# A normalisation stage with three token buffers, four turned-piece buffers, rounding on ScalarE, bias lines amid the tiles and the first weights requested inside it

## The chip, the cores and the metric

One core of one Trainium2 chip runs the whole program: TensorE (PE in the profile), VectorE (DVE), ScalarE (ACT), GpSimd (POOL) and SyncE (SP), with on-chip memories SBUF and PSUM and 16 DMA engines to the chip's main memory. The metric is the device time of one execution in microseconds; below, "span" is the time from the first to the last instruction of one profiled execution.

## The reference

A hybrid attention layer for 512 prompt tokens and 8 x 8 sample tokens, width 2048. What matters here is its head: every token is normalised and multiplied with a wide weight matrix, and a small table of bias values is spread over distances.

```python
def rmsnorm(x, g):
    xf = x.astype(jnp.float32)
    y = xf * lax.rsqrt(jnp.mean(xf * xf, axis=-1, keepdims=True) + EPS)
    return (y * g.astype(jnp.float32)).astype(x.dtype)
p = project(rmsnorm(x, g_pre), w_in)        # 576 tokens x 2048 by 2048 x 7510
bias = table[t5_bucket(distance)]           # 32 buckets x 12 heads, over 4231 distances
```

After it come the attention over a paged cache of 8 sequences, that of the prompt, an output projection and a second normalisation.

## The kernel before

The program is a row of stages, each a function with its own block of five instruction lists, one for each engine, written out by hand. Every wait is a semaphore wait at a place in such a list, and an engine runs its list strictly in order. Between two stages stands a barrier of all engines and a clearing of the stage's semaphores (`Scope.clear`, L161 to L164).

`setup_and_norm` (L167 to L304) is the first stage. The tokens are five tiles m of 128 rows (the last, the samples, has 64). For each tile:

- SP loads `norm_x` (1 MB), in two buffers; tile m waits until the four pieces of tile m-2 have been turned (L199).
- ACT squares and sums it (L235), DVE scales the sum (L278), ACT takes Ln and Exp (L239, L241) for the inverse root, DVE multiplies the tile by it (L280).
- PE turns it in four pieces q of 4 x 128 columns by transposes (L256) into `norm_tp` (PSUM, two buffers).
- DVE multiplies a turned piece by the gain column and writes `norm_hT` (L294, SBUF, two buffers).
- POOL rounds the piece to the first half `h_hi` (L223) and subtracts it from the piece for the second half `h_lo` (L225). For the samples both go to `h_s`.

DVE's list has the norm of tile m+1 ahead of the pieces of tile m. After the tiles PE makes nine bias line pieces (L265) into `norm_lp` (two buffers), ACT copies them to `norm_line` (L244), and SP stores the line (L206) and waits for its landing. DVE meanwhile clips and reorders the page numbers (L298 to L304).

`project_in` (L307 to L454) is the second stage: 15 column chunks of 512 (the last is narrower), each in four quarters q of the 2048 rows. SP loads a quarter of the weights (`proj_w`, 1 MB, L344), DVE rounds it (`proj_w_hi`, L360), POOL subtracts (`proj_w_lo`, L391), and PE does three products for each token tile and k (L422 to L424, for the samples L415 and L418). ACT copies the sums out (L446).

Of the kernel before, what the change touches and what calls it, by code (L numbers as in the profile page):

```python
# [24 lines left out]
P = 128  # L25
# [135 lines left out]
def setup_and_norm(nc, io, kept, h_hi, h_lo, h_s):  # L161


    with ExitStack() as ctx:  # L164
        s = Scope(nc, ctx, "norm")
        x = s.sb("x", [P, 2, D])
# [13 lines left out]
        x_in = [s.sem(f"x_in{i}") for i in range(2)]  # L180
# [8 lines left out]

        @block.sync  # L190
        def _(sp):
            sp.dma_start(kept.consts[:], io.consts[:, 0:C_KEPT]).then_inc(consts_in, 16)
            sp.dma_start(choices[:].rearrange("p a n -> p (a n)"), io.consts[:, C_SELE:C_PM]).then_inc(choices_in, 16)
            for m in range(5):
                if m >= 2:

                    sp.wait_ge(turned, 4 * (m - 1))
                src = io.xp[m * P:(m + 1) * P, :] if m < 4 else io.xs
                sp.dma_start(x[0:rows[m], m % 2, :], src).then_inc(x_in[m % 2], 16)  # L199
# [4 lines left out]

# [5 lines left out]
        def _(pool):  # L210
            with nc.allow_non_contiguous_dma(reason="a small column"):
                pool.dma_start(gcol[:], io.norm_pre.rearrange("(k p) -> p k", p=P)).then_inc(gain_in, 16)
            pool.wait_ge(gain_in, 16)
            for m in range(5):
                for q in range(4):
# [6 lines left out]
                    pool.wait_ge(hT_written, n + 1)  # L222
                    pool.tensor_copy(hi, hT[n % 2][:, :, 0:rows[m]]).then_inc(hi_made, 1)  # L223
                    pool.wait_ge(hi_made, n + 1)
                    pool.tensor_tensor(lo, hT[n % 2][:, :, 0:rows[m]], hi, ALU.subtract).then_inc(lo_made, 1)  # L225

        @block.scalar
        def _(act):
            act.preload_act_table_set("natural_log_exp_and_others")
            for m in range(5):  # L230
                act.wait_ge(x_in[m % 2], 16 * (m // 2 + 1))
                if m:

                    act.wait_ge(squared, m)
                act.activation(sq[0:rows[m], :], x[0:rows[m], m % 2, :], ACT.Square,  # L235
                               accum_out=ss[0:rows[m], m:m + 1]).then_inc(squared, 1)

# [4 lines left out]
            for n, (c, w) in enumerate(pieces):  # L242
                act.wait_ge(line_done, n + 1)
                act.copy(line[:, c:c + w], lp[n % 2][:, 0:w]).then_inc(line_copied, 1)  # L244

        @block.tensor
        def _(pe):
            pe.wait_ge(consts_in, 16)
            for m in range(5):
                pe.wait_ge(normed, m + 1)  # L250
                for q in range(4):
                    n = 4 * m + q
                    if n >= 2:
                        pe.wait_ge(hT_written, n - 1)
                    for k in range(4):
                        last = pe.transpose(tp[n % 2][:, k, 0:rows[m]], x[0:rows[m], m % 2, (4 * q + k) * P:(4 * q + k + 1) * P],  # L256
                                            kept.ident[0:rows[m], 0:rows[m]])
                    last.then_inc(turned, 1)

# [2276 lines left out]
```

## Time and profile before

| | |
|---|---|
| median of 3 runs | 3029.92 us (3025.42 to 3032.97) |
| profiled execution | 3023.38 us, span 3021.5 us, mean granted clock of PE 0.907 |
| busy: PE, DVE, ACT, POOL | 2406.0 us (80%), 1041.9 (34%), 757.9 (25%), 494.9 (16%) |
| VectorE's casts of constants (L271 to L273) | 0.43, 0.41 and 0.21 us |
| VectorE's page number operations (L298 to L304) | 61.92 us to 64.88 us |
| start of the bias line's store | 75.02 us |
| first matmul of the projection | 91.26 us |
| projection, matmuls | from 91.26 us to about 840 us |
| sizes of the first transfers | token tile 1024 KB, `norm_choices` 512 KB, constants 396 KB, `norm_onehot` 528.9 KB |

A row of the timeline has the start in us, the duration in us, the engine, the line, the operation, what it writes and reads, and the count of merged instructions; in brackets stands how long the engine had been idle before it and what ended that. "SPq" rows are the issuing of transfers, not their duration. A busy time is that of the engine's instructions alone; an engine that waits for another inside an instruction shows as busy.

### The profile page before, as it was taken

The page shows a single profiled execution, that of the slowest core. Times are in us where ns is not written, and L with a number is a line of the kernel's source. Part 1 is how long each engine was busy: PE and PEld are TensorE (multiplying, and loading weights), DVE is VectorE, ACT ScalarE, POOL GpSimd, SP SyncE. Part 2 cuts the span into 40 slices and gives each one's busy share as a digit, 9 for nine tenths or more (in the row PEclk, how much of TensorE's full clock was granted, in tenths as well). Part 3 has the DMA queues.
Part 4 walks back from the last instruction along what each step waited for, and adds up shares of the span by engine and source line. Part 5 has one row for each costly group of instructions (what it writes and reads, how often), then busy time and mean ns, then how long its engine had stood idle before and what let it go on. Part 6 is the DMA issues. An engine that isn't in the chain of part 4 may idle for free. (4 is left out here: it accounts for less than half of the span.)

```text
span 3021.5 us, 45203 instructions
## 1 busy us (share of the span) xinstructions
PE 2406.0 (80%) x16080; PEld 1792.4 (59%) x16080; DVE 1041.9 (34%) x1834; ACT 757.9 (25%) x1700; POOL 494.9 (16%) x338
## 2 busy tenths in 40 slices
PE   4799999999948888836858868888499453677996
PEld 2688888888838888832335534444255342555885
DVE  3211111010002221302248846766233259655413
ACT  2000000000012222210135434454255253344000
POOL 4533333333240000000000000000000000132431
PEclk9999999999979999967979978989799775898998
DMA  2523233232376363672289889999699460001323
GB/s 82 171 99 115 99 108 105 100 114 85 150 204 216 124 209 114 213 176 64 48 264 354 298 319 381 377 375 333 198 380 340 154 215 0 1 1 69 99 84 111
DMA packets 306803, 524.96 MB, mean 174 GB/s; under 512 B 63373, under 2 KB 80030, under 8 KB 304174
## 3 DMA queue, kind: packets, MB, share of 16 engines
q1 hardware_dynamic: 272442, 486.57, 47.2%
q10 hardware_dynamic: 31648, 31.64, 3.5%
q0 software_dynamic: 2560, 4.80, 0.5%
q8 instruction: 85, 1.39, 0.2%
q14 instruction: 68, 0.56, 0.1%
HBM read 500.65 MB, written 44.00 MB: 180 GB/s over the span
## 5 line engine op out<-in xcount | busy, mean ns | idle before, releaser
L422 PE MATMUL proj_acc<-proj_w_hi,h_hi 128*128 128x512 f32 (+1 forms) x960 | 370.0, 385 | 16.6 <-POOL proj_w_lo L391 16.6
L423 PE MATMUL proj_acc<-proj_w_hi,h_lo 128*128 128x512 f32 (+1 forms) x960 | 370.1, 386 | 0.0
L424 PE MATMUL proj_acc<-proj_w_lo,h_hi 128*128 128x512 f32 (+1 forms) x960 | 369.6, 385 | 0.0
L391 POOL TENSOR_TENSOR proj_w_lo<-proj_w,proj_w_hi 128x2048 fp32r<-128x2048 f32 (+1 forms) x60 | 272.0, 4534 | 476.2 <-DVE proj_w_hi L360 476.2
L360 DVE CAST proj_w_hi<-proj_w 128x2048 fp32r<-128x2048 f32 (+1 forms) x60 | 80.6, 1345 | 483.6 <-PE proj_acc L415 461.8
L664 PE MATMUL cmp_hp<-cmp_xT,cmp_w 128*128 128x128 f32 x2048 | 230.0, 275 | 0.0
L664 PEld LDWEIGHTS cmp_hp<-cmp_xT,cmp_w 128*128 128x128 f32 x2048 | 229.3, 192 | 0.0
L1186 PE MATMUL sb_tp<-kept_consts,sb_k_rows 128*128 128x128 f32 x1024 | 170.0, 316 | 64.1 <-DMA sb_k_rows<-in_cache_sb_kv_dram 47.1
L422 PEld LDWEIGHTS proj_acc<-proj_w_hi,h_hi 128*128 128x128 f32 x960 | 180.8, 188 | 52.7 <-issue 17.1
L446 ACT COPY proj_out<-proj_acc 128x512 f32<-128x512 f32 (+1 forms) x60 | 34.7, 579 | 705.6 <-PE proj_acc L424 705.6
L1186 PEld LDWEIGHTS sb_tp<-kept_consts,sb_k_rows 128*128 128x128 f32 x1024 | 127.2, 159 | 138.6 <-ACT sb_kT L1326 63.7
L423 PEld LDWEIGHTS proj_acc<-proj_w_hi,h_lo 128*128 128x128 f32 x960 | 180.8, 188 | 35.3
L424 PEld LDWEIGHTS proj_acc<-proj_w_lo,h_hi 128*128 128x128 f32 x960 | 180.7, 188 | 35.2
L1326 ACT COPY sb_kT<-sb_tp 128x512 f32<-128x512 f32 x256 | 144.5, 588 | 186.9 <-PE sb_tp L1186 186.4
L656 PE MATMUL cmp_tp<-kept_consts,cmp_rows 128*128 128x128 f32 x1040 | 134.0, 290 | 44.5 <-DMA cmp_rows<-in_cache_nsa_kv_dram 21.7
L656 PEld LDWEIGHTS cmp_tp<-kept_consts,cmp_rows 128*128 128x128 f32 x1040 | 125.0, 150 | 51.3 <-issue 26.7
L1480 DVE MAX8 kept_top<-scores 64x8 f32<-64x4104 f32 x32 | 141.5, 4422 | 1.0
L1482 DVE MATCH_REPLACE8 scores<-kept_top,scores 64x4104 f32<-64x4104 f32 x32 | 141.1, 4409 | 0.0
L722 DVE COPY cmp_xT<-cmp_tp 128x512 f32<-128x512 f32 x130 | 89.2, 691 | 72.0 <-PE cmp_tp L656 71.7
L2036 PE MATMUL pa_tp<-kept_consts,pa_logits 128*128 128x128 f32 x220 | 47.7, 322 | 82.5 <-DVE pa_logits L2174 55.3
L2345 PE MATMUL fin_acc<-fin_w_hi,fin_o_hi 128*128 128x512 f32 x256 | 100.9, 394 | 11.0 <-DVE fin_o_s L2401 11.0
L2346 PE MATMUL fin_acc<-fin_w_hi,fin_o_lo 128*128 128x512 f32 x256 | 100.6, 393 | 0.0
(398 smaller groups left out, 3599.7 us busy)
## 6 DMA issues: line engine op xcount, KB each, us to landing
cmp_rows<-in_cache_nsa_kv_dram SPq DMA_DIRECT2D x256, 256.0 KB, 5.2
slc_rows<-in_cache_nsa_kv_dram SPq DMA_DIRECT2D x256, 256.0 KB, 5.0
sb_k_rows<-in_cache_sb_kv_dram SPq DMA_DIRECT2D x256, 256.0 KB, 5.9
sb_v_rows<-in_cache_sb_kv_dram SPq DMA_DIRECT2D x256, 256.0 KB, 7.3
dsa_rows<-in_cache_dsa_kv_dram SPq DMA_DIRECT2D x256, 256.0 KB, 4.9
proj_w<-in_w_in_dram SPq DMA_DIRECT2D x56, 1024.0 KB
fin_w<-in_w_out_dram SPq DMA_DIRECT2D x32, 512.0 KB
proj<-proj_out ACTq DMA_DIRECT2D x14, 1024.0 KB, 4.4
```

What stands on the lines that cost most here:

```text
L391: pool.tensor_tensor(w_lo[q][:, :, 0:width], w[q][:, :, 0:width], w_hi[q][:, :, 0:width], ALU.subtract).then_inc(lo_made, 1)
L422: pe.matmul(to, h_hi[:, kk, r], w_hi[q][:, k, 0:width], start=(kk == 0), stop=False)
L423: pe.matmul(to, h_lo[:, kk, r], w_hi[q][:, k, 0:width], start=False, stop=False)
L424: last = pe.matmul(to, h_hi[:, kk, r], w_lo[q][:, k, 0:width], start=False, stop=(kk == KT_IN - 1))
L656: last = pe.transpose(tp[a][:, p * P:(p + 1) * P], rows[u][:, p, a, :], kept.ident)
L664: last = pe.matmul(hp[:, a, 0:blocks], w1[:, a, r, :], xT[:, a, r, 0:blocks], start=(r == 0), stop=(r == CMPB - 1))
L1186: last = pe.transpose(tp[j % 2][:, p * P:(p + 1) * P], here[:, p, h * DH:(h + 1) * DH], kept.ident)
L1326: act.copy(kT[(n * items + j) % KTS][:], tp[j % 2][:]).then_inc(kT_copied, 1)
L1480: dve.max(kept.top8[:], kept.scores[:]).then_inc(top_step, 1)
L1482: dve.match_replace(kept.scores[:], kept.top8[:], kept.scores[:], GONE).then_inc(top_step, 1)
L2345: pe.matmul(to[:], o_hi[:, h, r], hi[:, k, :], start=first, stop=False)
L2346: pe.matmul(to[:], o_lo[:, h, r], hi[:, k, :], start=False, stop=False)
```

## The change

The stage `setup_and_norm` is rewritten, and the first weight loads of `project_in` are moved into it.

- `norm_x` has three buffers, `norm_tp` and `norm_hT` four each.
- SP's list starts with the first two token tiles; the constants are loaded from ACT's queue, `norm_choices` from POOL's. After the last token tile SP requests the four quarters of the first weight chunk. The weight tensors `w_in0` to `w_in3` now live over both stages, and `project_in` loads from the second chunk on.
- ACT rounds the pieces (`split`), POOL only subtracts. ACT's list has the root of tile m+1 ahead of the rounding of tile m.
- The bias line pieces are made behind the tiles: two behind tiles 1, 2 and 3, three behind tile 4.
- DVE's three casts of constants stand after the tiles instead of first.

```diff
+def load_weights(sp, io, w, w_in, q, col, width):
+    Q = KT_IN // 4
+    sp.dma_start(w[q][:, :, 0:width], io.w_in[q * Q * P:(q + 1) * Q * P, col].rearrange("(k p) n -> p k n", p=P)).then_inc(w_in[q], 16)
...
-        x = s.sb("x", [P, 2, D])
+        XB, TB = 3, 4
+        x = s.sb("x", [P, XB, D])
...
-        hT = [s.sb(f"hT{i}", [P, 4, P]) for i in range(2)]
-        tp = [s.ps(f"tp{i}", [P, 4, P]) for i in range(2)]
+        hT = [s.sb(f"hT{i}", [P, 4, P]) for i in range(TB)]
+        tp = [s.ps(f"tp{i}", [P, 4, P]) for i in range(TB)]
...
+        behind = [(), (0, 1), (2, 3), (4, 5), (6, 7, 8)]
...
         def _(sp):
-            sp.dma_start(kept.consts[:], io.consts[:, 0:C_KEPT]).then_inc(consts_in, 16)
-            sp.dma_start(choices[:].rearrange("p a n -> p (a n)"), io.consts[:, C_SELE:C_PM]).then_inc(choices_in, 16)
             for m in range(5):
-                if m >= 2:
-
-                    sp.wait_ge(turned, 4 * (m - 1))
+                if m >= XB:
+
+                    sp.wait_ge(turned, 4 * (m - XB + 1))
...
+            for q in range(4):
+                load_weights(sp, io, w, w_in, q, slice(0, CH), CH)
             sp.wait_ge(line_copied, len(pieces))
...
-            pool.wait_ge(gain_in, 16)
+            pool.dma_start(choices[:].rearrange("p a n -> p (a n)"), io.consts[:, C_SELE:C_PM]).then_inc(choices_in, 16)
...
-                    pool.wait_ge(hT_written, n + 1)
-                    pool.tensor_copy(hi, hT[n % 2][:, :, 0:rows[m]]).then_inc(hi_made, 1)
                     pool.wait_ge(hi_made, n + 1)
-                    pool.tensor_tensor(lo, hT[n % 2][:, :, 0:rows[m]], hi, ALU.subtract).then_inc(lo_made, 1)
+                    pool.tensor_tensor(lo, hT[n % TB][:, :, 0:rows[m]], hi, ALU.subtract).then_inc(lo_made, 1)
...
         def _(act):
+            act.dma_start(kept.consts[:], io.consts[:, 0:C_KEPT]).then_inc(consts_in, 16)
...
+            root(0)
+            for m in range(5):
+                if m < 4:
+                    root(m + 1)
+                for q in range(4):
+                    split(4 * m + q)
+                for n in behind[m]:
+                    c, width = pieces[n]
+                    act.wait_ge(line_done, n + 1)
+                    act.copy(line[:, c:c + width], lp[n % 2][:, 0:width]).then_inc(line_copied, 1)
...
-                    if n >= 2:
-                        pe.wait_ge(hT_written, n - 1)
+                    if n >= TB:
+                        pe.wait_ge(hT_written, n - TB + 1)
...
+                for n in behind[m]:
+                    c, width = pieces[n]
+                    if n >= 2:
+                        pe.wait_ge(line_copied, n - 1)
+                    pe.matmul(lp[n % 2][:, 0:width], table[:], onehot[:, c:c + width], start=True, stop=True).then_inc(line_done, 1)
...
-            with sp.Fori(0, whole) as n:
+            with sp.Fori(1, whole) as n:
```

ScalarE's list, from its last root to the end of the stage; `norm_sq` is the square with its sum, `norm_rstd` the root, `norm_line` the copied bias line. Before:

```order
L235 ACTIVATE norm_sq,norm_ss<-norm_x 64x2048 [waits norm_squared,norm_x_in0]
L239 ACTIVATE norm_rstd<-norm_rstd 64x1 [waits norm_scaled]
L241 ACTIVATE norm_rstd<-norm_rstd 64x1 [waits norm_rooted]
L244 COPY norm_line<-norm_lp 12x512 [waits norm_line_done] x8
L244 COPY norm_line<-norm_lp 12x135 [waits norm_line_done]
```

With the change, from the same root on:

```order
L242 ACTIVATE norm_sq,norm_ss<-norm_x 64x2048 [waits norm_squared,norm_x_in1]
L245 ACTIVATE norm_rstd<-norm_rstd 64x1 [waits norm_scaled]
L247 ACTIVATE norm_rstd<-norm_rstd 64x1 [waits norm_rooted]
L254 CAST h_hi<-norm_hT 128x4x128 [waits norm_hT_written] x4
L265 COPY norm_line<-norm_lp 12x512 [waits norm_line_done] x2
L254 CAST h_s<-norm_hT 128x4x64 [waits norm_hT_written] x4
L265 COPY norm_line<-norm_lp 12x512 [waits norm_line_done] x2
L265 COPY norm_line<-norm_lp 12x135 [waits norm_line_done]
```

The rounding of the pieces has moved into this list, between the roots, and the line copies stand among it.

SyncE's list, the whole stage and the first load of the next. Before:

```order
L192 DMA kept_consts<-in_constants_dram 128x792
L193 DMA norm_choices<-in_constants_dram 128x1024
L199 DMA norm_x<-in_x_prompt_dram 128x2048 x2
L201 DMA norm_table<-in_rel_bias_dram 32x12
L202 DMA norm_onehot<-in_onehot_dram 32x4231
L203 DMA norm_table_rows<-in_page_table_dram 1x256
L199 DMA norm_x<-in_x_prompt_dram 128x2048 [waits norm_turned] x2
L199 DMA norm_x<-in_x_sample_dram 64x2048 [waits norm_turned]
L206 DMA bias_line<-norm_line 12x4231 [waits norm_line_copied]
```

With the change, the same stretch:

```order
L206 DMA norm_x<-in_x_prompt_dram 128x2048 x2
L208 DMA norm_table<-in_rel_bias_dram 32x12
L209 DMA norm_onehot<-in_onehot_dram 32x4231
L210 DMA norm_table_rows<-in_page_table_dram 1x256
L206 DMA norm_x<-in_x_prompt_dram 128x2048
L206 DMA norm_x<-in_x_prompt_dram 128x2048 [waits norm_turned]
L206 DMA norm_x<-in_x_sample_dram 64x2048 [waits norm_turned]
L163 DMA w_in<-in_w_in_dram 128x4x512 x4
L214 DMA bias_line<-norm_line 12x4231 [waits norm_line_copied]
```

The tokens are first, the third tile is asked for without a wait, and four weight loads stand ahead of the line's store.

TensorE's list at the end of the stage. Before:

```order
L256 MATMUL norm_tp<-kept_consts,norm_x 128x64 [waits norm_hT_written]
L256 MATMUL norm_tp<-kept_consts,norm_x 128x64 x3
L265 MATMUL norm_lp<-norm_onehot,norm_table 12x512 [waits norm_onehot_in,norm_table_in]
L265 MATMUL norm_lp<-norm_onehot,norm_table 12x512
L265 MATMUL norm_lp<-norm_onehot,norm_table 12x512 [waits norm_line_copied] x6
L265 MATMUL norm_lp<-norm_onehot,norm_table 12x135 [waits norm_line_copied]
```

With the change, from the line pieces behind tile 3 on:

```order
L287 MATMUL norm_lp<-norm_onehot,norm_table 12x512 [waits norm_line_copied] x2
L277 MATMUL norm_tp<-kept_consts,norm_x 128x64 [waits norm_hT_written,norm_normed]
L277 MATMUL norm_tp<-kept_consts,norm_x 128x64 x3
L277 MATMUL norm_tp<-kept_consts,norm_x 128x64 [waits norm_hT_written]
L277 MATMUL norm_tp<-kept_consts,norm_x 128x64 x3
L287 MATMUL norm_lp<-norm_onehot,norm_table 12x512 [waits norm_line_copied] x2
L287 MATMUL norm_lp<-norm_onehot,norm_table 12x135 [waits norm_line_copied]
```

Three of the nine pieces are left behind the last tile; the others have moved between the tiles.

## Rows read from the trace of the kernel before

**Rows 1.** The page's groups: busy, mean ns of one | idle before, releaser.

```profile
L422 PE MATMUL proj_acc<-proj_w_hi,h_hi 128*128 128x512 f32 (+1 forms) x960 | 370.0, 385 | 16.6 <-POOL proj_w_lo L391 16.6
...
L446 ACT COPY proj_out<-proj_acc 128x512 f32<-128x512 f32 (+1 forms) x60 | 34.7, 579 | 705.6 <-PE proj_acc L424 705.6
```

**Rows 2.** Windows by stage: busy us (count) of each engine, granted clock, DMA.

```profile
92.00:840.00 748.00, 748.00 (x3349) 610.87 (x3348) 83.82 (x73) 42.45 (x73) 267.50 (x59) 1.00 0.32 110
...
2500.00:3021.00 521.00, 392.35 (x1866) 303.53 (x1866) 269.66 (x863) 135.91 (x381) 137.16 (x157) 0.86 0.16 53
```

**Rows 3.** Timeline, 0 to 20 us.

```profile
0.73 0.40 SPq L192 DMA_DIRECT2D kept_consts<-in_constants_dram  x1
...
1.65 0.90 SPq L199 DMA_DIRECT2D norm_x<-in_x_prompt_dram  x2
...
9.36 1.91 ACT L235 ACTIVATE norm_sq<-norm_x 128x2048 f32<-128x2048 f32 x1 [7.35 <-DMA norm_x<-in_x_prompt_dram]
...
12.20 1.91 ACT L235 ACTIVATE norm_sq<-norm_x 128x2048 f32<-128x2048 f32 x1 [0.18 <-DMA norm_x<-in_x_prompt_dram]
...
16.17 1.28 DVE L294 TENSOR_TENSOR norm_hT<-norm_tp,norm_gcol 128x512 f32<-128x512 f32 x2
```

**Rows 4.** Windows of the first transfers; the last column is GB/s.

```profile
0.00:9.30 9.30, 0.00 (x0) 0.00 (x0) 0.89 (x3) 1.30 (x2) 1.58 (x5) 1.00 0.82 263
9.30:12.20 2.90, 0.00 (x0) 0.00 (x0) 0.30 (x2) 2.41 (x4) 0.00 (x0) 1.00 1.24 379
```

**Rows 5.** Timeline of the third token tile, up to the fourth's square.

```profile
20.96 0.69 DVE L294 TENSOR_TENSOR norm_hT<-norm_tp,norm_gcol 128x512 f32<-128x512 f32 x1 [1.22 <-POOL h_lo L225]
21.49 1.27 POOL L225 TENSOR_TENSOR h_lo<-norm_hT,h_hi 128x512 fp32r<-128x512 f32 x1
...
23.76 1.91 ACT L235 ACTIVATE norm_sq<-norm_x 128x2048 f32<-128x2048 f32 x1 [8.83 <-DMA norm_x<-in_x_prompt_dram]
...
26.45 1.28 DVE L280 TENSOR_SCALAR norm_x<-norm_x,norm_rstd 128x2048 f32<-128x2048 f32 x1 [0.50 <-ACT norm_rstd L241]
27.66 1.28 DVE L294 TENSOR_TENSOR norm_hT<-norm_tp,norm_gcol 128x512 f32<-128x512 f32 x2
...
28.39 1.97 PE L256 MATMUL norm_tp<-kept_consts,norm_x 128*128 128x128 f32 x8 [5.57 <-DVE norm_hT L294]
28.40 0.61 POOL L223 CAST h_hi<-norm_hT 128x512 fp32r<-128x512 f32 x1 [3.75 <-DVE norm_hT L294]
29.09 1.26 POOL L225 TENSOR_TENSOR h_lo<-norm_hT,h_hi 128x512 fp32r<-128x512 f32 x1
...
35.25 1.91 ACT L235 ACTIVATE norm_sq<-norm_x 128x2048 f32<-128x2048 f32 x1 [8.83 <-DMA norm_x<-in_x_prompt_dram]
```

**Rows 6.** Timeline from the last pieces to the projection's first matmul.

```profile
60.40 14.27 PE L265 MATMUL norm_lp<-norm_onehot,norm_table 32*12 32x512 f32 x18
...
74.25 0.74 ACT L244 COPY norm_line<-norm_lp 12x512 f32<-12x512 f32 x2 [1.13 <-PE norm_lp L265]
75.02 0.33 SPq L206 DMA_DIRECT2D bias_line<-norm_line  x1
80.19 45.44 SPq L344 DMA_DIRECT2D proj_w<-in_w_in_dram  x10
85.22 1.23 DVE L360 CAST proj_w_hi<-proj_w 128x2048 fp32r<-128x2048 f32 x1 [20.34 <-DMA proj_w<-in_w_in_dram]
86.63 4.49 POOL L391 TENSOR_TENSOR proj_w_lo<-proj_w,proj_w_hi 128x2048 fp32r<-128x2048 f32 x1 [22.80 <-DVE proj_w_hi L360]
...
91.26 0.79 PE L422 MATMUL proj_acc<-proj_w_hi,h_hi 128*128 128x512 f32 x1 [16.59 <-POOL proj_w_lo L391]
```

**Rows 7.** Timeline of VectorE and GpSimd around 93 us.

```profile
93.32 5.55 DVE L360 CAST proj_w_hi<-proj_w 128x2048 fp32r<-128x2048 f32 x1
...
92.36 5.43 POOL L391 TENSOR_TENSOR proj_w_lo<-proj_w,proj_w_hi 128x2048 fp32r<-128x2048 f32 x1 [1.24 <-DVE proj_w_hi L360]
```

**Rows 8.** The waits of the first 110 us, SyncE's queue: us in total, times, longest.

```profile
SPq L164 <- DMA bias_line<-norm_line: 3.5, 1, 3.5
```

More of the change, by code:

```diff
@@ L175, in setup_and_norm @@
         line = s.sb("line", [HB, LINE])
[L176 to L177 removed]
+        hT = [s.sb(f"hT{i}", [P, 4, P]) for i in range(TB)]
+        tp = [s.ps(f"tp{i}", [P, 4, P]) for i in range(TB)]
         lp = [s.ps(f"lp{i}", [HB, CH]) for i in range(2)]
         consts_in, gain_in, table_in, onehot_in = s.sem("consts_in"), s.sem("gain_in"), s.sem("table_in"), s.sem("onehot_in")
[L180 removed]
+        x_in = [s.sem(f"x_in{i}") for i in range(XB)]
         squared, rooted, scaled, normed = s.sem("squared"), s.sem("rooted"), s.sem("scaled"), s.sem("normed")
@@ L241, in _, with split @@
                 act.activation(rstd[0:rows[m], m:m + 1], rstd[0:rows[m], m:m + 1], ACT.Exp, scale=-0.5).then_inc(rooted, 1)
-            for n, (c, w) in enumerate(pieces):
-                act.wait_ge(line_done, n + 1)
-                act.copy(line[:, c:c + w], lp[n % 2][:, 0:w]).then_inc(line_copied, 1)
+            def split(n):
+                m, q = divmod(n, 4)
+                ks = slice(4 * q, 4 * q + 4)
+                hi = h_hi[:, ks, m * P:(m + 1) * P] if m < 4 else h_s[:, ks, 0, :]
+                act.wait_ge(hT_written, n + 1)
+                act.copy(hi, hT[n % TB][:, :, 0:rows[m]]).then_inc(hi_made, 1)
+            root(0)
[8 more added lines that the diff above has]
+                    act.copy(line[:, c:c + width], lp[n % 2][:, 0:width]).then_inc(line_copied, 1)
         @block.tensor
@@ L312, in project_in @@
         Q = KT_IN // 4
-        w = [s.sb(f"w{q}", [P, Q, CH]) for q in range(4)]
         w_hi = [s.sb(f"w_hi{q}", [P, Q, CH], F32R) for q in range(4)]
@@ L318, in project_in @@
         acc = [s.ps(f"acc{m}", [P, CH]) for m in range(5)]
-        w_in = [s.sem(f"w_in{q}") for q in range(4)]
         hi_made, lo_made, w_used, summed, copied = (s.sem(n) for n in ("hi_made", "lo_made", "w_used", "summed", "copied"))
@@ L2437, in program @@
               nc.sbuf_tensor("h_s", [P, KT_IN, 2, NS], F32R) as h_s):
-            setup_and_norm(nc, io, kept, h_hi, h_lo, h_s)
-            project_in(nc, io, h_hi, h_lo, h_s)
+            with ExitStack() as weights:
+                w = [weights.enter_context(nc.sbuf_tensor(f"w_in{q}", [P, KT_IN // 4, CH], F32)) for q in range(4)]
+                w_in = [s.sem(f"w_in{q}") for q in range(4)]
+                setup_and_norm(nc, io, kept, h_hi, h_lo, h_s, w, w_in)
+                project_in(nc, io, h_hi, h_lo, h_s, w, w_in)
         kept.cmp_kp = s.sb("cmp_kp", [P, 2, 16])
```

44 lines of the change are left out of this document (21 added, 23 removed).

## The prediction

> **What bounds the kernel now.** I read the page's groups first, then the windows by stage, then the timeline of the first 95 us. The projection's matmuls wait 16.6 us in all, for POOL's first subtract, and for nothing after it [rows 1]; from 92 to 840 us PE is busy for 748.00 of 748.00 us at a granted clock of 1.00 [rows 2]. So whatever makes the first matmul at 91.26 us start earlier shifts all that follows. The change touches only what stands ahead of it.
>
> The 91 us are one chain. The first two tiles wait for their loads: the squares start at 9.36 and 12.20, the first gain multiply at 16.17 [rows 3]. Then a tile takes 11.49 us (23.76 to 35.25), and ACT has been idle for 8.83 us of that until the tile's load lands, since the load is only asked for when the buffer has been turned [rows 5]. POOL rounds in 0.61 and subtracts in 1.26 us a piece. Behind the tiles stand the nine bias pieces with 14.27 us, the line's store at 75.02, its landing, a barrier, the weight load at 80.19, and from its landing cast, subtract and matmul at 85.22, 86.63 and 91.26 [rows 6].
>
> **The new chain, step by step.** I call H(m) the start of tile m's first gain multiply and work out each H.
>
> *H(0).* DVE has the norm of tile 1 ahead of it, so the load of tile 1 decides. By 9.3 us 9.3 x 263 GB/s = 2.45 MB had moved, while constants, choices and the first tile are 0.41 + 0.52 + 1.05 = 1.98 MB: 0.47 MB of later transfers had slipped ahead [rows 4]. Now tile 1 needs two tiles and the constants, 2.50 MB; with the same slip 2.97 MB, at 379 GB/s 1.4 us after 9.3, so at 10.7; if the choices share the way too, 3.50 MB and 12.1. I take 11.5. From that square to the first multiply went 16.17 - 12.20 = 4.0 us [rows 3], so H(0) = 15.5. Bounds: 2.50 MB and no slip gives 9.4 and 13.4; no gain at all gives 16.2.
>
> The Trainium skill ("DMA: Bandwidth & Descriptors", section "Issuing engines are not separate DMA queues") says that transfers asked for by SP, ACT and POOL interleave on the same 16 engines, so that other queues save issue time alone. By that rule moving constants and choices off SP's queue gives nothing but the place of the issue, and H(0) would be 16.2 less the 0.9 us of two issues. The 0.47 MB of slip in the row speaks for interleaving too, on one queue already.
>
> *One tile.* Four multiplies of 0.69 us, two in 1.28: the last ends at H + 2.65. ACT's rounding starts 0.14 us behind a multiply, as POOL's did (27.66 + 0.6 to 28.40) [rows 5]. What it takes on ACT no row shows. The nearest is its copy of the same 128x512 shape, 0.58 [rows 1]; bounds are a quarter of the 1.91 us square, 0.48, and POOL's 0.61. I take 0.60, so ACT has rounded at H + 3.4. Behind tiles 1 to 3 come two line copies, 1.2 us together. Then the next tile's square, long landed (it is asked for two tiles ahead), and from square to multiply 27.66 - 23.76 = 3.9 us. So a tile takes 7.3 us without line copies and 8.5 with them, against 11.49.
>
> *Locks.* VectorE's cast at 93.32 takes 5.55 us where it took 1.23 alone, since POOL's subtract ran until 97.79; and that subtract, begun at 92.36, takes 5.43 where 4.49 was its own, since VectorE's cast before it ran until 93.3 [rows 6, 7]. So a norm on DVE, an operation from SBUF to SBUF, must be expected to wait for a subtract that runs. The gain multiply reads PSUM: at 20.96 it keeps its 0.69 with a subtract beginning at 21.49, and the subtract keeps 1.27 [rows 5]. POOL's four subtracts start at about H + 1.5 and end at H + 6.5. The norm comes 1.3 us before the next H: at H + 6.1 without line copies, a wait of 0.4, and at H + 7.2 with them, none. Bounds: nothing, and a whole subtract (1.26) in each of the three steps.
>
> H(1) = 15.5 + 7.3 + 0.4 = 23.2, H(2) = 31.7, H(3) = 40.2. PE stays behind: a tile's 16 transposes at 0.25 us (8 in 1.97) and two pieces at 1.70 (the 14.27 us hold eight full pieces and a short one of 0.67) are 7.4 us of 8.5.
>
> *The tail.* Tile 4 needs no norm after tile 3. Tile 3's subtracts run one after another from 41.7 to 46.7 at 1.25 each. The last multiply waits for the last of them (four buffers) and ends at 47.1; its rounding ends at 47.7. Line copies 6 and 7 end at 48.9. Piece 8 may start when copy 6 has ended at 48.3 and takes 0.67; its short copy ends at 49.3. DVE's three casts (1.05 us) and page operations (64.88 - 61.92 = 3.0) come behind the last multiply and end at about 51 to 52, waits for subtracts included, before the store has landed at 52.8. So the store is asked for at 49.3, where it was 75.02: **25.7 us**.
>
> *The projection's start.* Its queue is free: the four weight loads, 4.2 MB, are asked for at about 20 us, 11 to 14 us at the rates of [rows 4], so the line's store behind them waits for nothing. From the store to the next stage stay 5.17 us (3.5 of them its landing [rows 8]). Weights being there, the 5.03 us from 80.19 to 85.22 go. But now VectorE's second cast follows the first at once, 0.2 us before POOL comes, so POOL's first subtract takes 5.5 instead of 4.49, as at 92.36 [rows 7]: 1.1 us back. In sum **3.9 us**. The later quarters each need 5.7 us (cast and subtract) against some 14 us of PE's work, and stay hidden.
>
> Sum: 25.7 + 3.9 = **29.6 us**, first matmul at 61.7. The profiled execution took 3023.38, so it would be 2993.8. That execution lies 6.5 us under the median of the runs; on the median's level the forecast is 3000.3, ratio 0.990.
>
> **The rivals.**
> - *The forecast*, gain 26 to 34: 65%.
> - *The multiply locks too.* What [rows 5] show overlaps by 0.16 us only. If a multiply waits for a subtract, the third and fourth of each tile do, some 1.3 us a tile over four tiles: 5 us less, gain 24, 3006. Against it speaks that even 0.16 us of shared time left no trace. 10%.
> - *Another engine paces.* PE has 1.1 us of slack a tile. If the waits in its list (a piece waits for its copy, the next tile for its norm) add 3 us a tile, the gain is 21, 3009. Against it: the copies of [rows 6] take a third of a piece. 11%.
> - *Faster than forecast*, gain over 34: it needs tile 1 by 9.4 (2.1), roundings of 0.48 (0.5), no locks (0.4 + 1.1) and half a microsecond a tile more. 6%.
> - *Weights not there in time* (the change does less than it says): the 5.0 us stay and POOL's 1.1 don't come, gain 25.7. It would take loads that wait for something other than their queue. 2%.
> - *The granted clock falls.* It was 1.00 in the projection but 0.86 in the last stage [rows 2], so it is not fixed by the program's text. Here all work moves 30 us earlier and nothing else changes; should the clock be granted 1.3% less over PE's 2406 busy us, it would cost 31 us and cancel the gain, more would make it slower (at 2%, 48 us: 3048). The three runs lie within 7.6 us, a quarter of that, so nothing like it has shown. 2%.
> - *Gain under 9 us*, by losses in later stages that no row here shows: 4%.
>
> **How the numbers follow.** The bounds around 29.6: H(0) +2.1 and -0.7, rounding +0.5 and -0.1, locks in the tiles +0.4 and -3.4, POOL's first subtract +1.1; together 25.4 to 33.7. With the two middle rivals down to 21, and some 3 us for the level of a median of three, the range is 2991 to 3011. Changes of more than 0.3% (9 us), about what a measurement of this kernel can tell from none: faster 0.94, within 0.04, slower 0.02.
>
> **What would show it.** In the changed profile: the square of tile 1 at 11 to 12 us; first multiplies of tiles 1, 2, 3 about 7.7, 8.5 and 8.5 us apart; ACT's casts at 0.6 us; subtracts back to back behind tile 3; the store at 49 us; VectorE's first projection cast 5.2 us after it; POOL's first subtract of 5.5 us; the first matmul at 62 us, and PE's idle time ahead of it 13 us where it was 16.6. Wrong would be: a norm or multiply much longer than 1.28 and 0.69, ACT waiting for a line piece or a load in the middle, a matmul in the projection that waits after the first, or any later stage whose length differs by more than a few microseconds.

## The result, and the profile after

The changed kernel takes 2999.98 us (median of 4 runs, 2996.70 to 3007.75), the kernel before 3028.54 us beside it: ratio 0.991, interval 0.9894 to 0.9927. Timed a second time it is 2996.61 us (median of 6 runs) against 3029.07 (11 runs), ratio 0.9893, interval 0.9873 to 0.9913. The gain is 28.6 and 32.5 us, about 1%; the forecast was 29.6 us and a time of 3000.3.

The page's first groups of the changed kernel (busy, mean ns of one | idle before, releaser) answer to [rows 1]. TensorE still waits once, ahead of its first projection matmul, now for 12.3 us:

```profile
span 2995.2 us, 45198 instructions
...
L441 PE MATMUL proj_acc<-proj_w_hi,h_hi 128*128 128x512 f32 (+1 forms) x960 | 370.3, 386 | 12.3 <-POOL proj_w_lo L410 12.3
```

The windows by stage, against [rows 2]: the projection is as before, full at a granted clock of 1.00.

```profile
0.00:61.00 61.00, 30.43 (x101) 16.70 (x102) 31.18 (x54) 28.39 (x51) 31.78 (x28) 0.67 0.56 175
61.00:810.00 749.00, 749.00 (x3353) 611.78 (x3353) 80.70 (x71) 42.62 (x74) 266.26 (x59) 1.00 0.32 110
...
2470.00:2995.00 525.00, 399.09 (x1866) 308.02 (x1866) 270.97 (x866) 136.28 (x381) 137.36 (x157) 0.85 0.16 53
```

The timeline of the changed kernel's first stage answers to [rows 3] and [rows 5]:

```profile
7.07 1.91 ACT L242 ACTIVATE norm_sq<-norm_x 128x2048 f32<-128x2048 f32 x1 [4.61 <-DMA norm_x<-in_x_prompt_dram]
...
11.78 1.91 ACT L242 ACTIVATE norm_sq<-norm_x 128x2048 f32<-128x2048 f32 x1 [2.05 <-DMA norm_x<-in_x_prompt_dram]
...
15.75 2.48 DVE L310 TENSOR_TENSOR norm_hT<-norm_tp,norm_gcol 128x512 f32<-128x512 f32 x4
16.47 2.41 ACT L254 CAST h_hi<-norm_hT 128x512 fp32r<-128x512 f32 x4 [1.95 <-DVE norm_hT L310]
...
17.18 4.95 POOL L231 TENSOR_TENSOR h_lo<-norm_hT,h_hi 128x512 fp32r<-128x512 f32 x4 [13.95 <-ACT h_hi L254]
...
18.79 1.91 ACT L242 ACTIVATE norm_sq<-norm_x 128x2048 f32<-128x2048 f32 x1
...
21.48 1.73 DVE L296 TENSOR_SCALAR norm_x<-norm_x,norm_rstd 128x2048 f32<-128x2048 f32 x1 [0.50 <-ACT norm_rstd L247]
23.13 2.47 DVE L310 TENSOR_TENSOR norm_hT<-norm_tp,norm_gcol 128x512 f32<-128x512 f32 x4
...
26.28 1.05 ACT L265 COPY norm_line<-norm_lp 12x512 f32<-12x512 f32 x2
...
31.13 2.48 DVE L310 TENSOR_TENSOR norm_hT<-norm_tp,norm_gcol 128x512 f32<-128x512 f32 x4
...
39.00 2.47 DVE L310 TENSOR_TENSOR norm_hT<-norm_tp,norm_gcol 128x512 f32<-128x512 f32 x4
```

The four multiplies of a tile stand in one piece (2.48 us), each with ACT's rounding behind it (2.41 for four) and POOL's subtract behind that (4.95 for four). From the third tile on no square waits for a load any more. The tiles start 7.38, 8.00 and 7.87 us apart, where a tile took 11.49. The one norm that lasts 1.73 us instead of 1.28 is the one that begins (21.48) while POOL's fourth subtract still runs (17.18 + 4.95 = 22.13).

The end of the stage answers to [rows 6]. The store is asked for at 47.79 us, not 75.02; the projection's first cast comes 5.09 us later, with its weights there; the first matmul stands at 59.73, not 91.26.

```profile
47.79 0.32 SPq L214 DMA_DIRECT2D bias_line<-norm_line  x1
...
52.88 13.29 DVE L379 CAST proj_w_hi<-w_in 128x2048 fp32r<-128x2048 f32 x4 [2.81 <-PEq L420]
54.28 16.34 POOL L410 TENSOR_TENSOR proj_w_lo<-w_in,proj_w_hi 128x2048 fp32r<-128x2048 f32 x3 [5.84 <-DVE proj_w_hi L379]
...
59.73 0.79 PE L441 MATMUL proj_acc<-proj_w_hi,h_hi 128*128 128x512 f32 x1 [12.26 <-POOL proj_w_lo L410]
```

So the start is 91.26 - 59.73 = 31.5 us shorter, but the two spans differ by 3021.5 - 2995.2 = 26.3 only. 5.3 us are missing in this pair of profiles. Whether the change costs them is the first question below; the others take the parts of the change one by one.

### The profile page after: what moved, and what is told of

It reads as the page before. It is cut to its first block and busy times, and to the rows that moved or that the text cites. A ratio compares the mean times of both kernels' runs of the same rounds, so it can differ in the third digit from the quotient of the medians.

```text
span 2995.2 us, 45198 instructions
## 1 busy us (share of the span) xinstructions
PE 2413.0 (81%) x16080; PEld 1801.1 (60%) x16080; DVE 1041.4 (35%) x1834; ACT 768.4 (26%) x1720; POOL 485.9 (16%) x319
## 5 line engine op out<-in xcount | busy, mean ns | idle before, releaser
L441 PE MATMUL proj_acc<-proj_w_hi,h_hi 128*128 128x512 f32 (+1 forms) x960 | 370.3, 386 | 12.3 <-POOL proj_w_lo L410 12.3
L410 POOL TENSOR_TENSOR proj_w_lo<-w_in,proj_w_hi 128x2048 fp32r<-128x2048 f32 (+1 forms) x60 | 273.0, 4552 | 459.7 <-DVE proj_w_hi L379 459.7
L379 DVE CAST proj_w_hi<-w_in 128x2048 fp32r<-128x2048 f32 (+1 forms) x60 | 80.3, 1343 | 467.8 <-PE proj_acc L434 465.0
L441 PEld LDWEIGHTS proj_acc<-proj_w_hi,h_hi 128*128 128x128 f32 x960 | 181.0, 189 | 48.4 <-issue 12.8
L2364 PE MATMUL fin_acc<-fin_w_hi,fin_o_hi 128*128 128x512 f32 x256 | 100.7, 393 | 10.8 <-DVE fin_o_s L2420 10.8
```

The lines of the kernel that those rows point to most:

```text
L410: pool.tensor_tensor(w_lo[q][:, :, 0:width], w[q][:, :, 0:width], w_hi[q][:, :, 0:width], ALU.subtract).then_inc(lo_made, 1)
L441: pe.matmul(to, h_hi[:, kk, r], w_hi[q][:, k, 0:width], start=(kk == 0), stop=False)
L2364: pe.matmul(to[:], o_hi[:, h, r], hi[:, k, :], start=first, stop=False)
```

## The experiments

In all of them the first matmul of the projection and the store of the bias line are the measure. They repeat well: the changed kernel's first matmul was at 59.73 and 59.84 us in two profiles, the kernel before's at 91.26 and 91.68. What does not repeat so well is the load of the second tile: its square starts anywhere from 11.43 to 12.37 us in the nine profiles whose first requests are those of the changed kernel, and all that follows shifts with it. So I also count from the first gain multiply behind that square, which is free of it: from there to the first matmul of the projection it is 43.98 us (59.73 - 15.75) and 43.99 (59.84 - 15.85) in the changed kernel's two profiles. I call this the chain behind the loads.

"Remainder" is the span less the first matmul. Ablations had one profiled execution each. Their total times aren't compared, since the remainder wanders by more than the parts are worth, as the table at the end shows.

**The weights' requests left out of the stage.**

```diff
-            for q in range(4):
-                load_weights(sp, io, w, w_in, q, slice(0, CH), CH)
             sp.wait_ge(line_copied, len(pieces))
...
-            with sp.Fori(1, whole) as n:
+            with sp.Fori(0, whole) as n:
```

> The changed kernel without its weight requests in the normalisation stage; they are asked for at the start of the projection, as before. My theory: the store of the bias line stays at 47.8 us, the load of 5.0 us comes back, and POOL's first subtract takes 4.5 us again instead of the 5.4 us that it takes beside VectorE's second cast; first matmul 59.7 + 5.0 - 1.0 = 63.7 us. Rival: the weights in flight had slowed the token loads or the line's store in the stage, then the store comes earlier here and the first matmul stands under 63 us.

The store stands at 47.62 and the first matmul at 64.04 us, 4.3 later than in the changed kernel; from store to matmul it is 16.42 instead of 11.94 us, 4.5 more. From the first gain multiply (15.56) to the store it is 32.06 us, as in the changed kernel (32.04), so the weights in flight cost the stage nothing. In the timeline of this kernel the cast waits again for the load, and POOL's first subtract is short:

```profile
58.00 1.23 DVE L377 CAST proj_w_hi<-w_in 128x2048 fp32r<-128x2048 f32 x1 [8.10 <-DMA w_in<-in_w_in_dram]
59.41 4.49 POOL L408 TENSOR_TENSOR proj_w_lo<-w_in,proj_w_hi 128x2048 fp32r<-128x2048 f32 x1 [11.13 <-DVE proj_w_hi L377]
```

**The weights' requests alone, in the kernel before.** The mirror of it: `load_weights` for four quarters behind the last token tile, the loads of `project_in` from the second chunk on, nothing else.

> The kernel before with this one part of the change: the first four weight loads are asked for behind the last token tile. My theory: the stage is unchanged, store at 75.0 us, first matmul at 91.26 - 5.0 + 1.0 = 87.3 us, with POOL's first subtract at 5.4 us. Rival: the full 5.0 us are won (86.3), the port being no matter.

The first matmul stands at 87.12 us, 4.1 earlier than 91.26 and 4.6 earlier than the 91.68 of the second profile of before. Store at 75.20, so from store to matmul it is 11.92 us instead of 16.24: 4.3 less. From this kernel's timeline:

```profile
80.27 13.30 DVE L365 CAST proj_w_hi<-w_in 128x2048 fp32r<-128x2048 f32 x4 [15.19 <-PEq L406]
...
87.12 0.79 PE L427 MATMUL proj_acc<-proj_w_hi,h_hi 128*128 128x512 f32 x1 [12.26 <-POOL proj_w_lo L396]
```

Cast to matmul is 6.85 us, where it was 6.04 in [rows 6]. The prefetch is worth 4.3 to 4.5 us, not the 5 of the load, in both kernels.

**The first chunk's other casts on ScalarE**, in the changed kernel, so that VectorE has no second cast to put ahead of POOL.

```diff
-            chunk(0, CH, None)
+            split(0, 0, CH)
+            dve.wait_ge(hi_made, 4)
...
+            for q in range(1, 4):
+                act.wait_ge(w_in[q], 16)
+                wait_used(act, q, 0)
+                act.wait_ge(hi_made, q)
+                act.copy(w_hi[q][:, :, 0:CH], w[q][:, :, 0:CH]).then_inc(hi_made, 1)
```

> The changed kernel with the first chunk's casts of quarters 1 to 3 on ScalarE instead of VectorE, nothing else. My theory: POOL's first subtract lasts 5.4 us beside VectorE's second cast and 4.5 without it; the first matmul comes 0.9 to 1.0 us earlier, at 58.8. Rival: the subtract is longer for another cause, such as where the weights now lie, and stays at 5.4.

First matmul at 58.72 us. From the cast at 52.65 it is 6.07 us, as in the kernel before; in the changed kernel it is 59.73 - 52.88 = 6.85. So the second cast cost 0.8 us, and the place of the weights nothing that shows.

**Two token buffers.** `XB, TB = 2, 4`.

> The changed kernel with two token buffers instead of three. My theory: with four turned-piece buffers a tile is turned right after its norm, so that the third tile is asked for at about 14.6 us, lands 4.8 us later, at 19.4, and is wanted at 18.8; the later ones land before they are wanted. Store 0.6 us later, at 48.4 us. Rival, the plain reading of the trace before, where ACT waited 8.8 us a tile for a load: the third buffer removes that wait, without it the store comes some 10 us or more later.

Store at 48.43 us, 0.64 later, as expected. But that is not the buffer's price. The second tile's square stands at 12.37 us here, 0.59 behind the changed kernel's 11.78, by its load alone and before a third buffer could matter. The third tile's square then waits 0.39 us for its load, which SP had asked for at 14.86 us:

```profile
12.37 1.91 ACT L242 ACTIVATE norm_sq<-norm_x 128x2048 f32<-128x2048 f32 x1 [2.66 <-DMA norm_x<-in_x_prompt_dram]
...
19.87 1.91 ACT L242 ACTIVATE norm_sq<-norm_x 128x2048 f32<-128x2048 f32 x1 [0.39 <-DMA norm_x<-in_x_prompt_dram]
...
22.56 1.29 DVE L296 TENSOR_SCALAR norm_x<-norm_x,norm_rstd 128x2048 f32<-128x2048 f32 x1 [0.50 <-ACT norm_rstd L247]
```

The norm behind it (22.56) comes after POOL's subtracts of the first tile and lasts 1.29 us, where the changed kernel's took 1.73 beside one, so the wait is won back. The chain behind the loads is 60.35 - 16.35 = 44.00 us, against 43.98: the third buffer is worth nothing that shows, and the expected 48.4 was met by luck.

No later square waits for a load. A load is asked for when the tile two before has been turned, and with four piece buffers turning is quick enough for two token buffers.

**Two turned-piece buffers.** `XB, TB = 3, 2`.

> The changed kernel with two turned-piece buffers (PSUM and SBUF) instead of four. My theory: the third and fourth multiply of a tile wait for the first and second subtract and end some 2 us later, three times ahead of the last tile, and the tail loses 2 more: store 8 us later, at 56 us, first matmul at 68. Rival: POOL's subtracts pace the stage anyway and two buffers lose under 2 us.

Store at 58.58 us, first matmul at 70.52: 10.8 us later, and 11.1 in the chain behind the loads (70.52 - 15.40 = 55.12). Tiles come 10.6 us apart (24.55, 35.18, 45.80). The multiplies fall apart in this kernel's timeline, and the line copies wait for their piece on top:

```profile
35.18 1.28 DVE L310 TENSOR_TENSOR norm_hT<-norm_tp,norm_gcol 128x512 f32<-128x512 f32 x2
...
37.97 0.69 DVE L310 TENSOR_TENSOR norm_hT<-norm_tp,norm_gcol 128x512 f32<-128x512 f32 x1 [1.51 <-PE norm_tp L277]
...
39.19 0.69 DVE L310 TENSOR_TENSOR norm_hT<-norm_tp,norm_gcol 128x512 f32<-128x512 f32 x1 [0.53 <-POOL h_lo L231]
...
41.44 0.57 ACT L265 COPY norm_line<-norm_lp 12x512 f32<-12x512 f32 x1 [0.43 <-PE norm_lp L287]
```

The last multiply ends 4.7 us behind the first, as worked out (2.2 later than with four). Of the 2.8 us beyond the expected 8 the row with the wait for a bias piece (0.43) shows a part, which I had not counted. Most of it is in the tail: from the last prompt tile's first multiply to the store it is 12.8 us (58.58 - 45.80) instead of 8.8, 4 more where I had put 2. Where in the tail they go I have not taken apart.

With three token buffers no square waits for a load here either, from the third tile on, and a tile still takes 10.6 us, near the 11.49 of before. So either kind of buffer ends the 8.83 us of waiting for a load in [rows 5], but beside the rest of the change only the piece buffers shorten the tile. What a third token buffer alone would be worth in the kernel before was not run. There ScalarE's list has no rounding ahead of the next square, so the two runs don't settle it.

**Rounding back on GpSimd.** `tensor_copy` of the piece in POOL's list ahead of the subtract, ACT's `split` left out.

> The changed kernel with the rounding of the pieces back on GpSimd. My theory: POOL then paces the stage with 16 pieces of 1.87 and 4 of 1.1 us and the norms' locks, 38 to 40 us from 16.5 on, and ends at 55 to 57 us, where it ended at 48.4; ACT is no longer in the chain of a tile. First matmul 4 to 6 us later, at 64 to 66 us. Rival: ACT's in-order list (rounding ahead of the next square) was the pace, and freeing it makes up for POOL: within 1 us of the changed kernel.

First matmul at 63.99 us, 4.3 later. POOL's last subtract ends at 55.06 instead of 48.44, while ACT is far ahead (squares at 17.75 and 22.87). The store is only 0.7 us later (48.52); what ends the stage is POOL. So moving the rounding is worth 4.3 us (4.0 in the chain behind the loads), and it shows behind the last tile rather than in the tiles, whose first multiplies even come earlier here (21.68, 28.38 and 36.99).

**All bias pieces behind the last tile.** `behind = [(), (), (), (), tuple(range(9))]`.

> The changed kernel with all nine bias pieces behind the last tile. My theory: each of three tiles is 1.0 us shorter, without the line copies in ACT's list, but the pieces take 14 us behind the last tile's transposes; store at about 53.8 us instead of 47.8, first matmul at 65.7. Rival: the pieces between the tiles cost PE and ACT as much as they save, store within 2 us.

Store at 57.62 us, first matmul at 69.56: 9.8 us later, of which 0.6 is a later load of the second tile (square at 12.36). The tiles are 7.37 us apart, shorter as expected, but each of the last three norms then lasts 1.72 to 1.74 us, since POOL's subtracts of the tile before are still running. The expected 53.8 was wrong. TensorE made two pieces at 41.58 and then waited for a buffer until 46.41, because the copies stand behind the last roundings in ACT's list.

**Constants and choices first on SyncE's queue again.** The two `dma_start` moved back ahead of the tokens.

> The changed kernel with the constants and the choices back at the head of SyncE's queue. My theory: transfers interleave whatever queue they are from, so the second tile's square moves from 11.8 us by half a microsecond, to about 12.3, and the first matmul by as much. Rival: the order in the queue sets it, 0.93 MB at 0.38 MB/us are 2.4 us, the square at 14.2 us.

The squares of the first two tiles stand at 9.48 and 12.30 us, the first multiply at 16.28, the first matmul at 60.39, 0.66 later. Asking for the tokens first brings the first tile 2.4 us earlier. For the second, on which the chain hangs, this pair says 0.5 us, but 12.30 lies within the 11.43 to 12.37 us at which that square stands with the tokens first, so all that can be said is that it is worth less than 1 us. The rival's 14.2 is out. The chain behind the loads is the same (60.39 - 16.28 = 44.11).

**The kernel before, a second profile.**

> The kernel before, unchanged, for a second profile. From its first projection matmul to the end of the span it took 2930.2 us in the first profile; the changed kernel took 2935.5. My theory: that length wanders by some 5 us from execution to execution, so another profile of before may stand anywhere from 2928 to 2942. Rival: the changed kernel's later stages are really slower by 5 us, and before stays within 1 us of 2930.

First matmul at 91.68, remainder 2929.6 us. That is within 1 us of 2930, as the rival had it, so this run speaks for the rival and doesn't show the wander that I expected, although 2929.6 fits both.

**The changed kernel again, with five rounds.**

> The changed kernel, unchanged, timed again. In nine other profiles the time from the first projection matmul to the end ran from 2921.0 to 2945.2 us, whichever kernel it was. My theory: that is wander of the later stages, in which a stretch runs at one or the other granted clock; the first matmul stands at 59.7 within 0.5 us again, while the remainder stands anywhere from 2925 to 2945, and the median gain over five rounds comes near the start's own 31.5 us (28 to 34). Rival: the change itself makes the later stages some 4 us longer, the gain stays at 27 to 28.

First matmul at 59.84, remainder 2934.0 us. The median gain is 3029.07 - 2996.61 = 32.5 us. The interval of the ratio (0.9873 to 0.9913, that is 26 to 38 us) doesn't exclude the rival's 27 to 28. Nor do the profiles: the changed kernel's two remainders (2935.5 and 2934.0) both lie some 4 to 6 us above the two of before. On the other side, the 10 runs of the changed kernel and the 15 of before beside them have medians 2997.36 and 3029.07, 31.7 us apart, just what the start gives. Whether the change costs the later stages a few us stays open.

**A version without the tail.** Three bias pieces behind each of tiles 1 to 3, with four buffers for them in PSUM; the line copies on VectorE behind its multiplies; VectorE's page operations and a cast between its first two norms; the first casts on ScalarE as above.

```diff
-        behind = [(), (0, 1), (2, 3), (4, 5), (6, 7, 8)]
+        behind = [(), (0, 1, 2), (3, 4, 5), (6, 7, 8), ()]
...
+                for n in behind[m]:
+                    c, width = pieces[n]
+                    dve.wait_ge(line_done, n + 1)
+                    dve.tensor_copy(line[:, c:c + width], lp[n % LB][:, 0:width]).then_inc(line_copied, 1)
```

> The changed kernel with the bias pieces three behind each of tiles 1 to 3, four bias buffers in PSUM, the line copies on VectorE in its idle time instead of ScalarE, VectorE's page operations and casts taken out of the tail, and the first chunk's casts of quarters 1 to 3 on ScalarE. My theory: tiles come 7.4 us apart instead of 8.0, the store lands before POOL's last subtract, which now ends the stage at about 47.4 us, and POOL's first projection subtract takes 4.5 instead of 5.4; first matmul at 54 to 56 us instead of 59.7, 4 to 5 us faster than the changed kernel over five rounds if the wander of the later stages lets it be seen. Rival: PE, with three pieces of 1.7 us and 3.65 us of transposes a tile, becomes the pace at 8.8 us a tile, and the first matmul stands at 59 us or later.

First matmul at 58.53 us, outside the expected 54 to 56 and short of the rival's 59; 2998.02 us (median of 6 runs), no better than the changed kernel beside it. The tiles are 7.4 us apart, but the second norm stands at 18.12 us instead of 14.55. VectorE's timeline of this kernel has the wait:

```profile
15.65 0.28 DVE L297 TENSOR_SCALAR kept_pages<-norm_table_rows 1x256 int32<-1x256 int32 x1 [4.12 <-DMA norm_table_rows<-in_page_table_dram]
```

A transfer of 1 KB, asked for at 2.7 us behind two token tiles and the one-hot table on SyncE's queue, landed at 15.6.

**The same with the page numbers first.** They are loaded ahead of the constants on ScalarE's queue, and the page operations stand ahead of VectorE's first norm, where it has nothing to do.

> The same as the kernel without a tail (bias pieces three behind a tile, copies on VectorE, first casts on ScalarE), but with the page numbers loaded first on ScalarE's queue and VectorE's page operations ahead of its first norm. In that kernel VectorE waited until 15.65 us for the page numbers, and the second norm ran at 18.1 us instead of 14.6. My theory: that wait was the whole loss of 3.5 us; the second norm is back at 14.6, the stage ends some 3.5 us earlier and the first projection matmul stands at 55.0 us, 4.7 before that of the changed kernel; in the median over five rounds 1 to 8 us faster than 2997, as the later stages wander. Rival: VectorE's line copies or TensorE's three pieces a tile hold the stage too, and the first matmul stays above 57 us.

First matmul at 53.54 us, 6.2 earlier than in the changed kernel, and 2986.44 us (median of 4 runs) against 3026.58 of before: ratio 0.9873, interval 0.9855 to 0.9892. Of the changed kernel's two intervals the first (from 0.9894) lies just above this one and the second overlaps it; the two were not timed beside each other. The first matmul is where the difference is plain. The timeline of this kernel's end of stage:

```profile
40.64 0.36 SPq L214 DMA_DIRECT2D bias_line<-norm_line  x1
...
43.43 2.75 POOL L231 TENSOR_TENSOR h_s<-norm_hT,h_s 128x256 fp32r<-128x256 f32 x4
...
47.48 1.23 DVE L381 CAST proj_w_hi<-w_in 128x2048 fp32r<-128x2048 f32 x1 [3.50 <-PEq L423]
...
53.54 0.79 PE L444 MATMUL proj_acc<-proj_w_hi,h_hi 128*128 128x512 f32 x1 [13.58 <-POOL proj_w_lo L413]
```

The stage is now ended by POOL's last subtract (46.2), no longer by the store and its landing. Of the 6.2 us some 1.3 are no merit of that: the token loads landed earlier (squares at 5.78 and 10.46), earlier than in any other profile. The constants came later instead (asked for at 1.30 us, behind the page numbers; TensorE's first transposes waited for them until 10.81). Whether the one made room for the other no run separates. In the chain behind the loads this kernel takes 53.54 - 14.44 = 39.10 us, 4.9 less than the changed one.

**Where the 5.3 us are.** The remainder, and the length of some stretches of it, over all profiles (from the first and last matmuls of the stages):

```text
kernel                 projection  compression  to selection  dsa to prompt  prompt   remainder
before                      750.4        427.1         240.1          165.3   264.7      2930.2
before, again               751.2        429.8         239.0          164.7   264.3      2929.6
weights alone in before     751.0        426.1         244.0          166.1   268.2      2938.7
changed                     751.0        429.3         244.5          163.1   267.0      2935.5
changed, again              750.3        431.7         245.6          162.6   262.2      2934.0
weights late                751.4        429.2         241.5          164.3   263.7      2929.7
two token buffers           751.2        429.9         245.2          171.1   264.6      2942.9
two piece buffers           750.3        428.9         244.3          171.2   269.5      2945.2
GpSimd rounds               750.6        428.2         244.5          165.7   262.1      2931.7
lines last                  750.5        423.4         242.0          164.7   261.9      2921.0
constants first             750.6        428.4         244.7          163.3   265.4      2932.3
first casts on ScalarE      750.4        431.4         245.3          169.7   263.7      2940.9
without the tail            750.9        424.4         243.6          166.2   264.6      2931.4
pages first                 750.7        425.0         241.9          166.3   265.5      2931.1
```

From the second chunk on the code of the later stages is the same in all of them, and the remainder runs over 24 us, from 2921.0 to 2945.2. The runs of one kernel range as far: 3020.29 to 3036.32 us for the 11 of before timed beside the changed kernel's second time.

TensorE's busy time goes with it. From the first projection matmul to the end, in the kernels with the shortest and the longest remainder (lines last, two piece buffers), in the columns of [rows 2]:

```profile
69.56:2990.60 2921.04, 2365.04 (x15979) 1771.46 (x15982) 1011.39 (x1782) 738.60 (x1669) 455.07 (x292) 0.91 0.52 176
70.52:3015.70 2945.18, 2397.10 (x15979) 1793.57 (x15982) 1012.54 (x1782) 739.43 (x1669) 455.10 (x292) 0.89 0.52 175
```

The same matmuls keep TensorE busy for 32 us longer at a lower mean clock, while the other engines' busy times differ by 1 us or so. One stretch shows how. It is 32 small matmuls of one line (`ca_ov`), in windows of that tile alone (PE, PEld, DVE busy, granted clock, DMA). In the changed kernel, first profile:

```profile
1339.50:1348.50 9.00, 7.03 (x32) 6.90 (x32) 1.52 (x16) 0.50 0.00 0
```

In the kernel before, first profile:

```profile
1369.00:1375.00 6.00, 4.27 (x32) 4.15 (x32) 1.53 (x16) 0.76 0.00 0
```

And the same line with the weights late, which is the changed kernel in all but its first 64 us (the tile's groups: duration ns min/median/max):

```profile
L1648 PE MATMUL ca_ov<-ca_pT,cmp_v x32: 269/269/388, 1343.7 to 1347.6; 128*128 128x24 f32 x32
```

With the weights alone in the kernel before:

```profile
L1636 PE MATMUL ca_ov<-ca_pT,cmp_v x32: 387/387/406, 1363.5 to 1370.1; 128*128 128x24 f32 x32
```

At a granted clock of 0.50, the lower of TensorE's two levels (1.2 GHz), the 32 matmuls take 387 ns each and 7.0 us in all; with the upper level (2.4 GHz) granted for a part of the window, 269 ns and 4.3 us. Both cases occur with the first stage of before and with the changed one. The median is 269 or 270 ns in both profiles of before, with the weights late, with the lines last and with the pages first; it is 387 or 388 ns in both profiles of the changed kernel, with the weights alone in before, and in the six other kernels. That is 2.8 us of the 5.3; the rest I have not taken apart. Each kernel that was profiled twice had the same level both times, so these profiles don't tell chance from a cause in the kernel's timing.

## Why the prediction was right

Point by point, its steps against the profile:

- *The load of the second tile decides the start.* Expected at 11.5, found 11.78; first multiply 15.75 for 15.5. The run with the constants first shows what the queues are worth: 2.4 us for the first tile, and for the second, on which the chain hangs, 0.5 us in that pair, no more than this square scatters (11.43 to 12.37). So that the forecast came within 0.3 us is partly luck. The Trainium skill ("DMA: Bandwidth & Descriptors", section "Issuing engines are not separate DMA queues") has it that transfers of all engines interleave and that another queue saves the time of issue alone. The second tile's 0.5 us is no more than the 0.9 of two issues; the first tile's 2.4 us is, so there the order in the queue counted too, and the measurement decides.
- *A tile's chain.* Expected 7.7, 8.5 and 8.5 us, found 7.38, 8.00 and 7.87. The rounding was sized well (0.60). I had put its whole 0.60 and 0.14 us behind a multiply block of 2.65; the block takes 2.48, and the square starts 3.04 us behind H instead of 3.4. Two line copies take 1.05 us, not 1.2, and the next square overlaps their end. These two sizes make the three tiles 1.45 us shorter than forecast (23.25 instead of 24.7). TensorE did not pace them: before the transposes of the last three tiles it stood idle for 0.79, 2.48 and 0.71 us, against a slack of 1.1 that I had worked out.
- *The lock.* Expected 0.4 us once, found 0.45 (1.73 instead of 1.28), in the tile without line copies and in no other norm. The run with the lines last, whose tiles all lack the copies, has it in each of its last three norms. The rival that multiplies lock too falls with the rows above: the third and fourth multiply run beside a subtract (from 17.18 on), and four still take 2.48 us, four subtracts 4.95.
- *The tail.* Copies and short piece came as worked out, 8.8 us from the last prompt tile's first multiply to the store (9.1 forecast). The store is at 47.79 instead of 49.3: 0.25 later by the loads, 1.45 earlier by the tiles, 0.3 by the tail.
- *The projection's start.* Expected 3.9 us, found 91.26 - 75.02 = 16.24 against 59.73 - 47.79 = 11.94, so 4.3. The price of VectorE's second cast is 0.8 us. I had put 1.1, more than the row I named shows (5.43 - 4.49 = 0.94).
- *PE is full from there on.* It is, 749.00 of 749.00 us. The "some 14 us" of PE's work for a quarter were too many: 751 us over 58.7 quarters (7510 columns) are 12.8, still more than twice the 5.7 of cast and subtract.
- *The granted clock.* Its mean fell from 0.907 to 0.896, and I had given a fall of 1.3% the price of the whole gain. That was wrong as a reading, since more than half of the fall is the first stage: recorded at 0.67 up to 61 us, at 1.00 in before, in work that doesn't hold the stage up. Without it the mean is 0.904 beside 0.901, as worked out from these figures. And that 1.00 can't be the level at which TensorE worked: in before a bias piece took 1.70 us, near the 1.8 that the changed kernel's profile has at 0.50, and not the 0.97 it has at 0.95. In the last stage the clock is 0.85 beside 0.86. But a wander of the later stages by up to 24 us between profiles was worth more than the 2% I gave it. One of my own signs of being wrong, a later stage that differs by more than a few microseconds, was there too: 244.5 us against 240.1 from compression to selection.
- *The range.* The bounds as added up, with the 3 us for the level, give 2993 to 3012 us; I wrote 2991 to 3011.

The forecast of 29.6 us lies between the two measured gains of 28.6 and 32.5, and the first of them is closer than the forecast earned. The start gave 31.5 to 31.8, some 2 us more than worked out: 1.5 by the store, 0.4 by the projection's start. The rest is the level of the later stages, which no step of the forecast covers.

By parts, each taken alone from the changed kernel and counted in the chain behind the loads: four piece buffers 11.1 us, bias pieces amid the tiles 9.3, weights 4.5, rounding on ScalarE 4.0, queue order 0.1, third token buffer 0.0. They add up to 29.0, near the 31.1 by which this chain is shorter than before's (91.26 - 16.17 = 75.09), though they overlap: without piece buffers, for instance, the bias pieces would stand in other gaps. One part was never taken alone, the three casts of constants behind the tiles instead of first.

## What to carry to other kernels

A wait that the profile puts down to a load may belong to whoever sets the load free: here ScalarE waited 8.8 us a tile for a transfer, and in the changed kernel four buffers for the turned pieces end that wait with two token buffers as well as with three. When a stage ahead of a saturated one is cut, work out each tile's chain from the timeline and compare first events, not total times, since one profile of the total wanders by more than most parts are worth. And compare them from an event behind the first loads: a part that seems to cost half a microsecond can be the scatter of a load. A prefetched operand can put a neighbour's second operation ahead of the first one that matters.

## What the runs showed that I had not expected

A 1 KB transfer asked for at 2.7 us behind larger ones on one queue landed at 15.6 us; asked for first on ScalarE's queue, at 0.73 us, it had landed at 2.0. TensorE was granted its lower level in parts of the first stage: windows of the changed kernel around two bias pieces each (PE, PEld, DVE, ACT, POOL busy, granted clock, DMA) read

```profile
19.50:23.20 3.70, 3.66 (x5) 0.38 (x4) 1.88 (x3) 1.69 (x4) 2.63 (x3) 0.50 0.55 149
27.50:29.50 2.00, 1.97 (x5) 0.29 (x4) 0.15 (x1) 1.78 (x3) 2.00 (x2) 0.95 1.05 387
```

so that two bias pieces took 3.6 us from 19.58 on and 1.9 us from 27.53 on, each time behind sixteen transposes. The second profile of the same kernel has it the other way round:

```profile
19.50:23.20 3.70, 2.24 (x8) 0.46 (x6) 1.78 (x2) 1.78 (x4) 2.73 (x3) 0.95 0.64 151
27.50:29.50 2.00, 2.00 (x4) 0.39 (x4) 0.13 (x1) 1.84 (x2) 2.00 (x2) 0.50 1.04 383
```

There the pair from 19.86 on took 1.88 us and that from 27.63 on 3.58, with the first projection matmul at 59.84 us instead of 59.73. So the instruction list alone doesn't decide the level, and here it costs nothing, since TensorE has time to spare. No run here was made to tell what decides it.
